# All transposes ahead of the attention heads on VectorE, head square sums on ScalarE, every fourth low weight part on GpSimd

## The reference

```
h = rms_norm(x);  z = h @ w_in          # z: sgu (u, v), q (8 heads), k, v (2 heads), memory q (4 heads), 3 gates
vs = rms_norm(gelu(v)) per group of 128; y_sgu = gelu(u) * (sgu_w @ vs + sgu_b)
q, k = rope(rms_norm(q) * q_norm), rope(rms_norm(k) * k_norm)          # per head of 128
y_attn = softmax(q k^T / sqrt(128)) v   # 8 query heads, 2 key heads
mq = rms_norm(mq) * mq_norm;  mk = rms_norm(mem part) * mk_norm
y_mem = softmax(mq mk^T / sqrt(128)) mv # 4 heads
y = sum of sigmoid(gate_i) * (branch_i @ w_br_i);  x = x + y @ w_out
x = x + (silu(a) * b) @ w_down          # a, b = rms_norm(x) @ w_gate_up
```

## Time and profile before

| | value |
|---|---|
| median of 3 runs | 2744.12 us |
| profiled execution, own time | 2744.39 us |
| its span | 2742.6 us |
| granted TensorE clock | 1.000 |
| TensorE busy | 2734.1 us (100%) |
| VectorE busy | 1813.4 us (66%) |
| ScalarE busy | 1242.0 us (45%) |
| GpSimd busy | 43.5 us (2%) |
| DMA | 195 GB/s mean |

### The profile page before, as it was taken

One profiled execution on the slowest core, in us unless ns is written; L12 is line 12 of the kernel. 1 busy time (PEld: TensorE's weight loads), 2 busy tenths in 40 slices (PEclk: granted clock), 3 DMA queues, 4 the chain that ended last, 5 costly groups with the idle time before them and its releaser, 6 DMA issues.

```text
span 2742.6 us, 29837 instructions
## 1 busy us (share of the span) xinstructions
PE 2734.1 (100%) x12178; PEld 2266.2 (83%) x12178; DVE 1813.4 (66%) x2302; ACT 1242.0 (45%) x1395; POOL 43.5 (2%) x60
## 2 busy tenths in 40 slices
PE   9999999999999999999999999999999999999999
PEld 7888888888888888888888888888888888888887
DVE  7875555677666476656878755556777665765665
ACT  6545444444444344434454454444444443444343
POOL 0001000000000000000000010000000000000000
PEclk9999999999999999999999999999999999999999
DMA  9554555555555556555555545555455555555553
GB/s 363 192 184 162 180 196 203 204 198 185 187 200 196 195 190 228 189 192 199 190 184 192 176 161 181 196 205 200 175 196 184 203 195 195 189 189 199 185 205 142
DMA packets 77657, 533.76 MB, mean 195 GB/s; under 512 B 8880, under 2 KB 8880, under 8 KB 14928
## 3 DMA queue, kind: packets, MB, share of 16 engines
q1 hardware_dynamic: 74800, 523.80, 53.5%
q0 software_dynamic: 2288, 7.47, 1.0%
q10 hardware_dynamic: 432, 0.58, 0.1%
HBM read 529.72 MB, written 2.10 MB: 194 GB/s over the span
## 4 chain that ended last, share of the span: by engine, by line
PE 99%; DVE 1%; DMA 0%; ACT 0%; DVEq 0%; POOL 0%; issue 0%; SPq 0%; ACTq 0%
PE acc L360 32%; PE acc L362 32%; PE acc L361 32%; PE tr L451 1%; PE acc L419 1%; PE tr L387 1%; PE tr L434 0%; DVE w_lo L895 0%; DMA raw<-weights 0%; PE acc L489 0%; ACT w_hi L605 0%; POOL rows L313 0%; DVE rows L1010 0%; DVE stats L989 0%; ACT rows L669 0%
## 5 line engine op out<-in xcount | busy, mean ns | idle before, releaser
L895 DVE TENSOR_TENSOR w_lo<-raw,w_hi 128x1024 fp32r<-128x1024 f32 x975 | 1189.3, 1225 | 872.3 <-ACT w_hi L605 864.4
L605 ACT ACTIVATE w_hi<-raw 128x1024 fp32r<-128x1024 f32 x975 | 1030.4, 1060 | 1373.6 <-PE acc L362 1369.2
L360 PE MATMUL acc<-w_hi,b_hi 128*128 128x512 f32 x1952 | 763.5, 391 | 2.4 <-DVE b_lo L931 1.3
L360 PE MATMUL acc<-w_hi,a_hi 128*128 128x512 f32 x1952 | 763.6, 391 | 0.0
L362 PE MATMUL acc<-w_hi,a_lo 128*128 128x512 f32 x1952 | 759.7, 389 | 0.0
L362 PE MATMUL acc<-w_hi,b_lo 128*128 128x512 f32 x1952 | 759.6, 389 | 0.0
L361 PE MATMUL acc<-w_lo,a_hi 128*128 128x512 f32 x1952 | 759.5, 389 | 0.0
L361 PE MATMUL acc<-w_lo,b_hi 128*128 128x512 f32 x1952 | 759.5, 389 | 0.0
L360 PEld LDWEIGHTS acc<-w_hi,b_hi 128*128 128x128 f32 x1952 | 366.5, 188 | 78.8 <-DVE b_lo L931 1.8
L362 PEld LDWEIGHTS acc<-w_hi,b_lo 128*128 128x128 f32 x1952 | 366.5, 188 | 76.4
L362 PEld LDWEIGHTS acc<-w_hi,a_lo 128*128 128x128 f32 x1952 | 366.5, 188 | 76.3
(11 more groups left out here) (111 smaller groups left out, 696.3 us busy)
## 6 DMA issues: line engine op xcount, KB each, us to landing
raw<-weights SPq DMA_DIRECT2D x484, 1024.0 KB, 4.8
bias<-bias_in POOLq DMA_DIRECT2D x24, 256.0 KB, 4.3
raw<-weights SPq DMA_DIRECT2D x7, 512.0 KB, 9.5
y<-memT_in SPq DMA_DIRECT2D x14, 256.0 KB, 6.9
rows<-mem_in SPq DMA_DIRECT2D x1, 2048.0 KB, 15.9
x<-xT_in SPq DMA_DIRECT2D x1, 2048.0 KB, 20.1
x<-x_in SPq DMA_DIRECT2D x1, 2048.0 KB, 7.4
out<-x SPq DMA_DIRECT2D x3, 512.0 KB, 7.3
```

The source lines that it names most:

```text
L360: pe.matmul(o, hi[:, kt + k, tok], wh, start=first and k == 0, stop=False)
L605: act.activation(w_hi[:, h % SPLIT_SLOTS, :], raw[:, slot, part * HALF:(part + 1) * HALF], ACT.Copy).then_inc(hi_ready, 1)
L895: dve.tensor_tensor(w_lo[:, h % SPLIT_SLOTS, :], raw[:, slot, part * HALF:(part + 1) * HALF], w_hi[:, h % SPLIT_SLOTS, :].bitcast(F32), AL ...
```

## The change

- TensorE's transposes of the rows of u, keys, memory queries and both halves of the queries are gone. VectorE turns u into `tr` with `turn`, and the keys, memory queries and queries with a new `turn_heads` straight into `kT`, `mem_qT` and `qT` in SBUF. TensorE waits on a new semaphore `heads_turned` ahead of heads 0, 4 and 8.
- `take_out` of chunks 4 to 7 is all on ScalarE, and takes square sums, head by head, from PSUM in front of the copies. VectorE's `take_scaled` and `head_sums` of these chunks are gone; the query roots are one `rsqrt` of 24 columns instead of three of 8. ScalarE's `turn_out` of keys and queries is gone. The memory query's gain is multiplied into the memory key's gain.
- From half 24 on, halves whose number in the layer is a multiple of 4, except 64 to 103, get their low part from GpSimd, counted by `pool_lo`. `split_to` places them in GpSimd's list ahead of its other work.

```diff
+HEADS_AT = 8 * FULL
+POOL_FROM = 3 * FULL
+BIAS_FREE = [HEADS_AT + FULL * c + 4 for c in range(1, NC + 1)]
+for c_ in range(NC - 1):
+    BIAS_FREE += [HEADS_AT + FULL * (5 + 3 * c_) + 4, HEADS_AT + FULL * (5 + 3 * c_) + 11]
+def on_pool(h):
+    r = h % (2 * N_UNITS)
+    return h >= POOL_FROM and r % 4 == 0 and not HEADS_AT <= r < HEADS_AT + (NC + 1) * FULL
...
 def load_unit(u):
-                sp.wait_ge(lo_ready, 2 * (u - RAW_SLOTS) + 2)
+                freed = 2 * (u - RAW_SLOTS) + 2
+                sp.wait_ge(lo_ready, freed - pool_before(freed))
+                if on_pool(freed - 2):
+                    sp.wait_ge(pool_lo, pool_before(freed))
...
+            def split_to(position):
+                while n.n.get("half", 0) < position:
+                    h = n.n.get("half", 0)
+                    if on_pool(h):
+                        pool.wait_ge(hi_ready, h + 1)
+                        pool.tensor_tensor(w_lo[:, h % SPLIT_SLOTS, :],
+                                           raw[:, h // 2 % RAW_SLOTS, h % 2 * HALF:(h % 2 + 1) * HALF],
+                                           w_hi[:, h % SPLIT_SLOTS, :].bitcast(F32), ALU.subtract
+                                           ).then_inc(pool_lo, 1)
+                    n.add("half")
...
+                at = layer * 2 * N_UNITS
                 for a in range(N_HEADS):
+                    split_to(at + HEADS_AT + 2 * a + 10)
                     scale_head(a)
...
                 for k in range(5, N_BRANCH * NC):
+                    split_to(at + BIAS_FREE[k - 2] + 1)
                     load_bias(k, layer)
+                split_to(at + 2 * N_UNITS)
...
+                    elif k == 0 and on_pool(at):
+                        pe.wait_ge(pool_lo, pool_before(at + 1))
...
-                chunk(1, *A, upto=1)
-                wait_rows()
-                transposes(rows_at(R_U))
-                chunk(1, *A, first=1)
...
+                    if i in (1, 1 + N_MEM, 1 + N_MEM + GROUP):
+                        n.add("turned_in", 2 if i == 1 else 1)
+                        pe.wait_ge(heads_turned, n.at("turned_in"))
...
+            def take_out(acc_i, r, func, sums=None, spare=None):
                 chunk_done(4)
+                if sums is not None:
+                    heads = sums.shape[1] // TB
+                    for t in range(TB):
+                        for g in range(heads):
+                            act.activation(rows[:, spare, t, g * HD:(g + 1) * HD],
+                                           acc[acc_i][:, t, g * HD:(g + 1) * HD], ACT.Square,
+                                           scale=rs_x[:, t:t + 1], accum_out=sums[:, t * heads + g:t * heads + g + 1])
...
+                split(4)
+                take_out(0, R_KV, ACT.Copy, kv_ss, R_TMP)
+                split(3)
+                op_plain(m_hi[:, 0:SGU_G, :])
                 split(5)
+                take_out(1, R_MQ, ACT.Copy, q_ss[:, 0:8], R_Q)
+                split(8)
+                take_out(0, R_Q, ACT.Copy, q_ss[:, 8:16], R_TMP)
                 split(4)
...
                     if s == 3:
+                        take_out(1, R_Q + 1, ACT.Copy, q_ss[:, 16:24], R_V)
...
+            def turn_heads(dst, of, part):
+                for pq in range(QUADS):
+                    src = of[pq * SQ:(pq + 1) * SQ, :, :].rearrange("p t (k f i) -> p t k f i", f=QUADS, i=SQ)
+                    to = dst[part * SQ:(part + 1) * SQ, :, :].rearrange("p k (t q i) -> p t k q i", t=TB, q=QUADS)
+                    last = dve.transpose(to[:, :, :, pq, :], src[:, :, :, part, :])
+                return last
...
+                turn(rows_of(R_U), 0)
+                split(1)
+                turn(rows_of(R_U), 1)
+                split(1)
+                turn(rows_of(R_U), 2)
+                split(1)
+                wait_taken(0)
+                rsqrt(rs[:, 0:TB * N_KV], kv_ss, HD)
                 dve.drain()
                 head_norm(R_KV, N_KV)
+                split(1)
+                turn(rows_of(R_U), 3)
                 dve.drain()
                 split(1)
+                rotate(R_KV, R_V, R_Q, 2, N_KV)
+                split(1)
+                op_plain(slice(0, SGU_G))
+                split(1)
+                dve.drain()
+                for part in range(QUADS):
+                    last = turn_heads(kT, rows[:, R_KV, :, 0:N_KV * HD], part)
+                    if part % 2 == 1:
+                        split(1)
+                last.then_inc(heads_turned, 1)
+                split(2)
+                wait_taken(1)
+                for part in range(QUADS):
+                    split(1)
+                    last = turn_heads(mem_qT, rows_of(R_MQ), part)
+                last.then_inc(heads_turned, 1)
                 split(4)
+                wait_taken(0)
+                rotate(R_Q, R_V, R_TMP, 0, 4)
+                split(1)
                 dve.drain()
+                turn_heads(qT[:, 0:GROUP, :], rows_of(R_Q), 0)
+                split(1)
+                turn_heads(qT[:, 0:GROUP, :], rows_of(R_Q), 1)
                 split(1)
                 for s in range((NC + 1) * FULL):
                     split(1)
+                    if s in (0, 2):
+                        last = turn_heads(qT[:, 0:GROUP, :], rows_of(R_Q), 2 + s // 2)
...
                     if s == 5:
+                        rsqrt(q_scale.rearrange("p g t h -> p (g t h)"), q_ss, HD, SCALE)
                     if s == 6:
+                        rotate(R_Q + 1, R_V, R_Q, 0, 4)
+                        dve.drain()
+                    if s in (8, 10, 12, 14):
+                        last = turn_heads(qT[:, GROUP:N_Q, :], rows_of(R_Q + 1), s // 2 - 4)
```

More of the change, by code:

```diff
@@ L118, with pool_before @@
 N_VEC = V_SGUB + SGU_G
+HEADS_AT = 8 * FULL
[6 more added lines that the diff above has]
+    return h >= POOL_FROM and r % 4 == 0 and not HEADS_AT <= r < HEADS_AT + (NC + 1) * FULL
+POOL_HALVES = [h for h in range(DEPTH * 2 * N_UNITS) if on_pool(h)]
+def pool_before(h):
+    return sum(1 for p_ in POOL_HALVES if p_ < h)
 class Counts:
@@ L203, in trunk @@
         op_hi = sem("op_hi")
+        heads_turned = sem("heads_turned")
         mem_ready, head_ready = sem("mem_ready"), sem("head_ready")
@@ L493, in _ @@
                 chunk(0, *A, first=6)
-                chunk(1, *A, upto=1)
-                wait_rows()
-                transposes(rows_at(R_U))
-                chunk(1, *A, first=1)
[L500 to L511, removed]
+                chunk(1, *A)
+                n.add("tr")
+                chunk(0, *A)
+                chunk(1, *A)
                 for i in range(NC * UNIT_KT):
@@ L894, in split @@
                     dve.wait_ge(hi_ready, n.at("half", 1))
-                    dve.tensor_tensor(w_lo[:, h % SPLIT_SLOTS, :], raw[:, slot, part * HALF:(part + 1) * HALF],
-                                      w_hi[:, h % SPLIT_SLOTS, :].bitcast(F32), ALU.subtract).then_inc(lo_ready, 1)
+                    if not on_pool(h):
+                        dve.tensor_tensor(w_lo[:, h % SPLIT_SLOTS, :], raw[:, slot, part * HALF:(part + 1) * HALF],
+                                          w_hi[:, h % SPLIT_SLOTS, :].bitcast(F32), ALU.subtract
+                                          ).then_inc(lo_ready, 1)
                     n.add("half")
@@ L1177, in _ @@
                     rsqrt(rs_x, ss_x, D).then_inc(rs_ready, 1)
+                dve.tensor_tensor(vecs_all[:, layer, V_MK:V_MK + 1], vecs_all[:, layer, V_MK:V_MK + 1],
+                                  vecs_all[:, layer, V_MQ:V_MQ + 1], ALU.mult)
                 turn(rows_of(R_MK), 0)
@@ L1212, in _ @@
                                                     in1=u_, op0=ALU.add, op1=ALU.mult)
-                last.then_inc(rows_ready, 1)
-                n.add("tr", 5)
-                split(2)
-                take_scaled(0, rows[:, R_KV, :, :], rs_x)
+                turn(rows_of(R_U), 0)
[6 more added lines that the diff above has]
+                rsqrt(rs[:, 0:TB * N_KV], kv_ss, HD)
@@ L1226, in _ @@
                 split(1)
-                rotate(R_KV, R_V, R_Q, 2, N_KV).then_inc(rows_ready, 1)
-                split(1)
-                split(4)
-                take_scaled(1, rows[:, R_MQ, :, :], rs_x)
-                dve.drain()
-                split(1)
-                head_sums(R_MQ, R_V)
-                split(1)
-                rsqrt(q_scale[:, 0, :, :].rearrange("p t h -> p (t h)"), ss[:, 0:8], HD, SCALE)
-                split(2)
-                split(5)
-                wait_taken(0)
```

44 lines of the change are left out of this document (11 added, 33 removed).

## The result

The changed kernel takes 2748.26 us (2747.50 to 2749.09, 20 runs) against 2744.17 before (20 runs): ratio 1.0014, 95% interval 1.0008 to 1.0020. It is 4.1 us slower, where 1.5 us faster was forecast (2742.9 against the 2744.4 of the profiled execution). The profiled execution took 2748.6 us, with a span of 2746.8 us.

What follows compares the result with a forecast made beforehand. The prediction took TensorE to bound the kernel (99% of the chain). From 2744.4 us, -8.1 + 0.7 + 1.2 + 1.4 + 3.3 = -1.5 gave 2742.9 us, with a range of 2737.5 to 2750.

Steps and rivals of the forecast that it cites:

- (b): Halves 44 to 50, both layers: half 47 late if GpSimd goes first at half 48; +0.6 a layer, 1.2 us.
- (a): Halves 27 to 31, layer 0: GpSimd's halves 24 and 28 hold rsqrt steps; 0 to 1.9 late, taken +0.7 us.
- (c): Halves 60 to 63, both layers: squares, rotation and one hold make low parts late; +0.7 a layer, 1.4 us.
- (d): First head, both layers: low part 73 late, TensorE's probability turn due earlier; +1.65 a layer, 3.3 us.
- Transposes: Row transposes taken off TensorE, four groups of 8 and one of 4 per layer: -8.1 us, all on the path.
- GpSimd's low part: A 128x1024 low part on GpSimd takes 2.1 us (1.8 to 3.9), net cost up to 1.0 where VectorE is behind.
- (e): Everywhere else: VectorE mostly waits for ScalarE, margin stays 2 us or more, possible table load taken as 0; nothing lost.
- second rival: Holds decide: GpSimd gets the ports first, holding one-input operations too wherever VectorE has a backlog; up to 2753.8 us, chance 0.17.
- the forecast by itself: The main case, about even with the kernel before, no rival true: 2739 to 2748 us, chance 0.63.

Runs made afterwards that it cites:

- experiment 10: On experiment 9, a low part placed behind each of the keys' four quarter turns instead of each second: 2737.57 us, 0.9975.
- experiment 1: The changed kernel with all low parts back on VectorE, transposes and squares as changed: 2740.51 us, 0.9986.
- experiment 3: The changed kernel with GpSimd's low parts only from half 104 of each layer on: 2740.48 us, 0.9985.
- experiment 2: The kernel before with only GpSimd's low parts added, transposes staying on TensorE: 2746.31 us, 1.0007.
- experiments 4 to 6: The changed kernel with low parts given back to VectorE: halves 24, 28, 48, then also 44, then also 52, 60: 2745.59, 2744.53, 2741.60 us.
- experiment 6: The changed kernel with halves 24, 28 (layer 0) and 44, 48, 52, 60 (both layers) back on VectorE: 2741.60 us, 0.9993.
- experiment 9: On experiment 3, the last queries' four quarter turns one head later: 2739.24 us, 0.9982.
- experiment 11: On experiment 10, the first of the last queries' late quarter turns put ahead of low part 74: 2737.58 us, 0.9975.
- experiment 12: On experiment 1, four low parts repeated six to eight times more to make TensorE wait on purpose: 2762.13 us, 1.0064, 4 runs.

## Why the prediction was wrong

The direction was wrong; the mechanism and the four places were right, and two terms were mis-sized. The sum had 6.6 us lost, the account has 12.4: of the 5.8 between, (b) is 4.8, (a) 1.6 and (c) 0.2, less 0.8 of (d).

- **Transposes, -8.1.** Right as far as the runs tell. That the account closes with 8.1 is no test, since it puts them in; but where nothing else was lost (experiment 10, (b) and (c)) it comes out within 0.15, and TensorE's busy time is 5.9 to 7.5 us less in experiments 1, 3 and 10. Into SBUF the 32 x 256 ones cost 436 ns (456 taken).
- **GpSimd's low part.** 2.40 us against 2.1 taken (ends 1.8 to 3.9), so a hold costs up to 1.26 net, not 1.0. The figure of the Trainium skill, GPSIMD Engine Reference, section 3.1, 4497 ns for 2048 elements, halves to an estimate of 2.25 us: nearer, still below.
- **(a), +0.7.** Measured 2.3 in the after-profile and 2.2 in experiment 2, above even the worst of 1.9, though up to 1 us of one profile can be scatter. I took the middle of a range whose condition (half 28's high part is done while rsqrt runs) could be read from the timeline before: ready 78.5, rsqrt until 78.2 and 0.5 later with half 24's hold. So the hold was the case to expect, not one of two alike.
- **(b), +1.2: the step that failed.** Measured 6.0. It weighed one contest, at half 48, half and half. GpSimd won it in both layers: it asked while the first addition of the rotation's end ran and came in behind it, ahead of the second, which was ready. And experiments 4 to 6 show that half 48 was not the one main term, for VectorE is behind over the whole stretch and carries each hold on. Given back to VectorE one after another, half 48 took 0.5 us off (b) in layer 0 and 1.4 in layer 1 (there mostly the clock's), half 44 1.1 and 0.4, half 52 nothing and 0.6. Beside the holds stand 0.4 to 0.8 us a layer of VectorE's own backlog (two key turns in a row, experiment 10), that I had as met, and 1.4 of TensorE's clock (layer 1), for which there was no term at all.
- **(c), +1.4.** Measured 1.6; experiment 6 puts 1.4 of it on half 60's hold, as forecast. GpSimd came in behind the first operation after the shared start, and the low end (0 without a hold) is what experiment 1 shows, 0.1 a layer. Eight squares take 2.74 us (2.9 taken).
- **(d), +3.3.** Measured 2.5. The place and both causes were right: the quarter turn between low parts 72 and 73 (experiment 9 takes it away) and the scaling that meets low part 74 (experiment 11).
- **(e), nothing.** Right for GpSimd's 192 low parts behind the heads (experiment 3), and for the table load: the traces before and after have seven each. The second rival's further condition, that one-input operations are held too, is wrong for transposes and PSUM operands, and right for `TENSOR_SCALAR` within SBUF, which I had among the free ones by my rule.
- The measured 2748.26 lies inside 2737.5 to 2750, but above the 2739 to 2748 of the forecast by itself: it is the wider range, stretched for the second rival, that holds it, and that is no merit of the sum. The second rival's point of decision, over 8.1 us lost, was reached with 12.4, by the holds together with the first head (2.5), VectorE's backlog (1.0) and the clock (1.4); its 17.5 was not. I had given it 0.17.

Open are two things: how much of the spread of 2747.5 to 2749.1 us is the clock's echo, and what decides between the two engines when both ask at once. In both layers, at halves 48 and 60, it was GpSimd that came in, with VectorE's next operation ready, and it never waited for a second one. At half 28 GpSimd simply began first, 0.09 us ahead. Why a `TENSOR_SCALAR` within SBUF is held and a transpose isn't, no run shows.

## What to carry to other kernels

Work on GpSimd with two SBUF inputs isn't beside VectorE's work of that kind, it is in its queue: price it as a stop of VectorE of its full length wherever VectorE is behind and works on SBUF inputs, and put it only where VectorE waits for somebody else (where it cost nothing here, and brought nothing either). Read the margin of each deadline (end of the producing operation to start of the consumer) over the whole kernel before moving work; a mean load of 66% said nothing here. Where an engine is behind over several deadlines, add all holds in the stretch, not the one that is nearest to the deadline.

## What the runs showed of the hardware

- GpSimd subtracts two 128 x 1024 float32 tiles in 2.40 us (median of 218), VectorE in 1.23. While either runs, the other's operation with two SBUF inputs does not: steps of 0.16 us took 2.32 on VectorE, and on GpSimd a scaling of 1.04 us took 1.94.
- A `TENSOR_SCALAR` from SBUF to SBUF was held until GpSimd's end too (1.72 and 2.23 us instead of 0.17). The Trainium skill, GPSIMD Engine Reference, section 1 (Specifications), names instructions in a 2-port mode beside those with two inputs; these holds would fit that, but no run shows in which mode the step ran.
- 32 x 256 transposes from SBUF to SBUF take 436 ns and were not held; nor were transposes into PSUM (456 ns) or the forms with one input in PSUM (738 and 1218 ns).
- GpSimd's operations were never delayed by more than 1.07 us, and never by a second VectorE operation behind the running one, while VectorE's low parts waited up to 2.2 us for one of GpSimd's (3.43 us instead of 1.23).
- After the six waits of TensorE of 1.9 to 4.7 us (one in the changed kernel, one in experiment 6, four in experiment 12) it worked at 1.2 GHz for 2.6 to 4.3 us, at 1.4 to 2.4 us of loss; after all waits of 1.0 to 1.8 us past the first 20 us of these traces it kept 2.4 GHz. That the length of the wait alone decides was not shown. The Trainium skill, TensorE: Matmul & The Clock Gate, Part 1, says that this clock gate passes the full or the half rate and nothing between; the 0.227 and 0.43 us between matmuls agree.
